# A ring of eight weight slots in place of six for the experts of a two-block model, with the item loop written out for four placements

## The reference, cut to what matters

```
logits = h @ router_w + router_b               # 256 tokens, 32 experts
top_val, top_idx = top_k(logits, 4)            # 4 experts a token
gate = softmax(top_val)
for each expert e, for its tokens x:
    gu  = x @ w_gu[e] + b_gu[e]                # 1024 -> 2048
    g, up = split(gu); g = min(g, 7); up = clip(up, -7, 7)
    act = (up + 1) * (g * sigmoid(1.702 * g))
    y[token] += gate * (act @ w_down[e] + b_down[e])   # 1024 -> 1024
h = h + g2 * rmsnorm(y, ffn_post_g)
```

## Time and profile before

| | us |
|---|---|
| median of 3 runs (lowest, highest) | 1937.54 (1937.01, 1938.84) |
| the profiled execution's own time | 1938.65 |
| its span | 1936.9 |
| TensorE busy | 1864.7 |
| VectorE busy | 768.5 |
| ScalarE busy | 231.1 |
| GpSimd busy | 207.3 |
| data moved by the DMA queues | 558.10 MB, mean 288 GB/s |

### The profile page before, as it was taken

One profiled execution on the slowest core, in us unless ns is written; L12 is line 12 of the kernel. 1 busy time (PEld: TensorE's weight loads), 2 busy tenths in 40 slices (PEclk: granted clock), 3 DMA queues, 4 the chain that ended last, 5 costly groups with the idle time before them and its releaser, 6 DMA issues.

```text
span 1936.9 us, 23084 instructions
## 1 busy us (share of the span) xinstructions
PE 1864.7 (96%) x8340; PEld 912.3 (47%) x8340; DVE 768.5 (40%) x1594; ACT 231.1 (12%) x466; POOL 207.3 (11%) x397
## 2 busy tenths in 40 slices
PE   7999999999999999999999999999999999999996
PEld 4466777754667777655433333323323333332332
DVE  3553111145535773395633323323223323332334
ACT  1421000014110000231110000000000000000001
POOL 0200000002006868321000000000000000000000
PEclk9999999999999999999899999999999999999999
DMA  8143343241448865225399999999997499999995
GB/s 310 65 172 117 152 159 147 109 186 65 174 189 323 326 264 199 87 87 228 152 428 428 429 429 428 428 428 429 428 429 292 202 429 429 428 428 428 429 429 236
DMA packets 40910, 558.10 MB, mean 288 GB/s; under 512 B 4534, under 2 KB 5430, under 8 KB 6364
## 3 DMA queue, kind: packets, MB, share of 16 engines
q1 hardware_dynamic: 40380, 556.06, 69.5%
q10 hardware_dynamic: 480, 1.37, 0.2%
HBM read 556.35 MB, written 1.06 MB: 288 GB/s over the span
## 4 chain that ended last, share of the span: by engine, by line
PE 65%; DMA 23%; DVE 9%; issue 2%; ACT 1%; POOL 0%; SPq 0%; ACTq 0%; DVEq 0%; POOLq 0%
DMA ring<-in_exp_w 23%; PE PS L1746 15%; PE PS L2048 15%; PE PS L1474 8%; PE PS L1765 8%; PE PS L2079 6%; PE PS L1651 3%; PE PS L1936 1%; PE PS L2034 1%; PE PS L2056 1%; DVE ring L1151 1%; DVE tT L1389 1%; DVE tT L1392 1%; DVE tb L1393 1%; DVE tb L1390 1%
## 5 line engine op out<-in xcount | busy, mean ns | idle before, releaser
L2048 PE MATMUL PS<-ring,tb 128*64 128x512 f32 x2176 | 481.5, 595 | 22.7 <-POOLq L2188 20.2
L2048 PEld LDWEIGHTS PS<-ring,tb 128*64 128x64 f32 x2176 | 150.5, 137 | 349.5 <-issue 295.8
L1746 PE MATMUL PS<-hT,ring 128*128 128x256 f32 x1376 | 300.6, 379 | 0.0
L1746 PEld LDWEIGHTS PS<-hT,ring 128*128 128x128 f32 x1376 | 261.1, 190 | 43.0 <-issue 8.6
L2079 PE MATMUL PS<-ring,tb 128*64 128x512 f32 x1088 | 241.0, 595 | 3.7
L1474 PE MATMUL PS<-ring,hT 128*128 128x512 f32 (+2 forms) x448 | 187.6, 561 | 3.4 <-ACT hT L420 3.3
L1389 DVE TENSOR_SCALAR tT<-PS 128x512 f32<-128x512 f32 x34 | 23.5, 692 | 397.5 <-PE PS L2056 397.5
L1765 PE MATMUL PS<-ring,tT 128*128 128x512 f32 x352 | 154.7, 593 | 0.0
L2079 PEld LDWEIGHTS PS<-ring,tb 128*64 128x64 f32 x1088 | 77.7, 137 | 145.1 <-issue 143.9
L1078 DVE TENSOR_TENSOR tT<-PS,tT 128x512 f32<-128x512 f32 x22 | 15.2, 692 | 270.3 <-PE PS L1746 270.3
L1474 PEld LDWEIGHTS PS<-ring,hT 128*128 128x128 f32 x448 | 81.7, 192 | 72.2 <-issue 60.0
(11 more groups left out here) (449 smaller groups left out, 1584.5 us busy)
## 6 DMA issues: line engine op xcount, KB each, us to landing
ring<-in_exp_w SPq DMA_DIRECT2D x192, 2048.0 KB, 21.2
ring<-in_w_gate_up SPq DMA_DIRECT2D x22, 2048.0 KB, 8.5
ring<-in_ada_w SPq DMA_DIRECT2D x12, 2048.0 KB, 9.3
ring<-in_w_in_part SPq DMA_DIRECT2D x10, 2048.0 KB, 10.1
ring<-in_w_down SPq DMA_DIRECT2D x10, 2048.0 KB, 7.3
ring<-in_w_out SPq DMA_DIRECT2D x6, 2048.0 KB, 8.6
ring<-in_w_in SPq DMA_DIRECT2D x4, 2048.0 KB, 8.1
ring<-in_w_in_part SPq DMA_DIRECT2D x2, 1608.0 KB, 11.8
```

What stands on the lines that cost most here:

```text
L1746: ins = pe.matmul(PS[:, 4 + 2 * (i % 2) + part, 256 * f:256 * f + 256], wt[:, k, 256 * part + 128 * f:256 * part + 128 * f + 128], hT[:, k ...
L2048: ins = pe.matmul(PS[64 * h:64 * h + 64, b, :], xg[:, o:o + 64], ring[:, s, w:w + 512], start=k == 0, stop=False, skip_group_check=True)
```

## The change

1. `ring`, `xn` and `proj` become one tensor `mega`, one behind the other, under their old names. The first 32768 columns are eight places of 4096: six are the ring, the seventh covers `xn` and the first 2048 columns of `proj`, the eighth the next 4096 columns of `proj`. The regions inside `proj` change their order: `post`, then `g_row`, then `p2`.
2. Load s of expert e goes to place (6e + s) mod 8. The pattern repeats after four experts. The load before it in that place is slot (s + 4) mod 6 of expert e - 1, or of e - 2 for s = 0 and 1, and SP waits for that one to be freed. SP also waits until the previous load counted on the same semaphore has landed. SP's loop over the experts is written out.
3. Expert 1's load 0 is issued once the S5 gate's products are through and expert 0's load 0 has landed; its load 1 after the bias product L2023, the item counts, and a copy by POOL of the second half of `g_row` to a free part of the constants (`g_ffn`), from where the final norm now reads it.
4. TensorE's loop becomes an outer loop of eight trips over four copies of the item's code, one for each expert mod 4; each copy is an inner loop from the item count of the expert before to that of the expert, and both are read from the table with `value_load`.
5. Other users of the memory move: the squares' scratch output goes to `junk` in the constants and later to `tb`, the gathered rows `xr` to `par`, the comparison for the items' experts is made in two halves in `tmp`, the total is read from `item_i[95]`, and `item_i[63]` becomes 0. The `idle_products` read another part of the constants.

```
+        mega = sb("mega", [P, 4096 * RING + TT * D + TT * IN_W])
+        ring = mega[:, 0:4096 * RING].rearrange("p (s n) -> p s n", s=RING)
...
+        def slot_of(r, s):
+            at = 4096 * ((6 * r + s) % SLOTS)
+            return mega[:, at:at + 4096]
...
-            expert(0, 0)
+            for s in FIRST_ORDER:
+                sp.wait_ge(freed[s], USES_BEFORE[s] + 1)
+                sp.dma_start(slot_of(0, s), a["exp_w"][0, s]).then_inc(landed[s], 16)
+            sp.wait_ge(g.pe2, PE2["gl_p"] + 1)
+            sp.wait_ge(landed[0], 16 * LOADS_BEFORE[0] + 16)
+            sp.dma_start(slot_of(1, 0), a["exp_w"][1, 0]).then_inc(landed[0], 16)
+            sp.wait_ge(g.pe2, PE2["m_bd"] + 1)
+            sp.wait_ge(g.u_pa, 7)
             sp.wait_ge(g.dve2, DVE2["m_cnt"] + 1)
-            with sp.Fori(1, N_EXPERTS) as e:
-                expert(e, sp.value_load(item_i[0:1, bass.ds(e + ENDS_AT - 1, 1)], min_val=1, max_val=MAX_ITEMS))
+            sp.wait_ge(landed[1], 16 * LOADS_BEFORE[1] + 16)
+            sp.dma_start(slot_of(1, 1), a["exp_w"][1, 1]).then_inc(landed[1], 16)
...
+            for e in range(1, N_EXPERTS):
+                before, done = done, items_until(e - 1)
+                for s in range(2 if e == 1 else 0, RING):
+                    last = (s + 4) % RING
+                    sp.wait_ge(freed[last], (before if s < 2 else done) + (USES_BEFORE[last] + 1))
+                    sp.wait_ge(landed[s], 16 * (e + LOADS_BEFORE[s]))
+                    sp.dma_start(slot_of(e % SLOT_TURNS, s), a["exp_w"][e, s]).then_inc(landed[s], 16)
...
-            with pe.Fori(0, items) as n:
+            def item(n, r):
...
+            def items_until(e):
+                return pe.value_load(item_i[0:1, bass.ds(e + ENDS_AT, 1)], min_val=0, max_val=MAX_ITEMS)
+            with pe.Fori(0, N_EXPERTS // SLOT_TURNS) as m:
+                for r in range(SLOT_TURNS):
+                    with pe.Fori(items_until(SLOT_TURNS * m + (r - 1)), items_until(SLOT_TURNS * m + r)) as n:
+                        item(n, r)
...
+            pool.wait_ge(g.dve2, DVE2["s5_d"] + 1)
+            link.to(pool.tensor_copy(g_ffn, g_row[:, 1024:2048]), g.u_pa, 7)
```

More of the change, by code:

```diff
@@ L153 @@
 FIRST_ORDER = (3, 2, 4, 5, 0, 1)
+SLOTS, SLOT_TURNS = 8, 4
 def last_plan():
@@ L273, in program @@
         pf = proj[:, :, :].rearrange("p t c -> p (t c)")
-        p2 = pf[:, 0:Q_N]
-        g_row = pf[:, Q_N:Q_N + 2048]
-        post = pf[:, Q_N + 2048:Q_N + 4096]
+        post = pf[:, 0:2048]
+        g_row = pf[:, 2048:4096]
+        p2 = pf[:, 4096:4096 + Q_N]
+        g_ffn = K[:, K_DEC:K_DEC + 1024]
+        junk = K[:, K_DEC + 1024:K_DEC + 1536]
         ssm = tbf[:, 0:2048].rearrange("p (i n) -> p i n", i=4)
@@ L385, in _ @@
                     sp.dma_start(bias_in.rearrange("p (h t) -> p h t", h=NH), rows).then_inc(g.s_b2, 16)
[L387 to L391, removed]
-            expert(0, 0)
-            sp.wait_ge(g.dve2, DVE2["m_cnt"] + 1)
-            with sp.Fori(1, N_EXPERTS) as e:
-                expert(e, sp.value_load(item_i[0:1, bass.ds(e + ENDS_AT - 1, 1)], min_val=1, max_val=MAX_ITEMS))
+            for s in FIRST_ORDER:
[6 more added lines that the diff above has]
+            sp.wait_ge(g.u_pa, 7)
+            sp.wait_ge(g.dve2, DVE2["m_cnt"] + 1)
+            sp.wait_ge(landed[1], 16 * LOADS_BEFORE[1] + 16)
+            sp.dma_start(slot_of(1, 1), a["exp_w"][1, 1]).then_inc(landed[1], 16)
+            def items_until(e):
+                return sp.value_load(item_i[0:1, ENDS_AT + e:ENDS_AT + e + 1], min_val=1, max_val=MAX_ITEMS)
+            done = None
+            for e in range(1, N_EXPERTS):
[5 more added lines that the diff above has]
+                    sp.dma_start(slot_of(e % SLOT_TURNS, s), a["exp_w"][e, s]).then_inc(landed[s], 16)
             for t in range(TT):
@@ L651, in mixed_squares @@
                 s = st[:, 246 + 2 * t + nh:247 + 2 * t + nh]
-                link.to(nc.scalar.activation(xn[:, t, 512 * nh:512 * nh + 512], PS[:, 2 + 2 * t + nh, :], ACT.Square, accum_out=s),
+                link.to(nc.scalar.activation(junk, PS[:, 2 + 2 * t + nh, :], ACT.Square, accum_out=s),
                         g.act2, ACT2[f"w_s1_{t}"] + nh + 1)
@@ L658, in residual_squares @@
                     s = st[:, 250 + 2 * t + nh:251 + 2 * t + nh]
-                    link.to(nc.scalar.activation(xn[:, t, 512 * nh:512 * nh + 512], x[:, t, 512 * nh:512 * nh + 512], ACT.Square, accum_out=s),
+                    link.to(nc.scalar.activation(junk, x[:, t, 512 * nh:512 * nh + 512], ACT.Square, accum_out=s),
                             g.act2, ACT2[f"w_s2_{t}"] + nh + 1)
@@ L686, in _ @@
             act.wait_ge(g.dve2, DVE2["m_cnt"] + 1)
-            items = act.value_load(item_i[0:1, 63:64], min_val=N_EXPERTS, max_val=MAX_ITEMS)
+            items = act.value_load(item_i[0:1, ENDS_AT + 31:ENDS_AT + 32], min_val=N_EXPERTS, max_val=MAX_ITEMS)
             with act.Fori(0, items) as n:
@@ L701, in _ @@
                 act.wait_ge(g.m_f, t + 1)
-                nc.scalar.activation(xn[:, t, :], oacc[:, t, :], ACT.Square, accum_out=st[:, 230 + t:231 + t]).then_inc(g.m_fs, 1)
+                nc.scalar.activation(tbf[:, 1024 * t:1024 * t + 1024], oacc[:, t, :], ACT.Square, accum_out=st[:, 230 + t:231 + t]).then_inc(g.m_fs, 1)
         @block.vector
@@ L1355, in _ @@
             modulated(link, 1)
[L1357 to L1360, removed]
+            half = MAX_ITEMS // 2
+            below = tmp[:, 512:512 + 32 * half].rearrange("p (j e) -> p j e", j=half)
+            for j in (0, half):
+                link(v.tensor_tensor(below, tmp[:, 32:64].unsqueeze(1).broadcast_to([P, half, 32]),
+                                     K[:, K_IOTA + j:K_IOTA + j + half].unsqueeze(2).broadcast_to([P, half, 32]), ALU.is_le))
+                link(v.tensor_reduce(owner[:, j:j + half], below, AX_X, ALU.add))
             link(v.tensor_scalar(owner, owner, float(N_EXPERTS - 1), None, ALU.min))
@@ L1363, in _ @@
             link.to(v.tensor_copy(item_i[:, MAX_ITEMS:MAX_ITEMS + 1], owner[:, MAX_ITEMS - 1:MAX_ITEMS]), g.dve2, DVE2["m_tab"] + 1)
-            items = v.value_load(item_i[0:1, 63:64], min_val=N_EXPERTS, max_val=MAX_ITEMS)
+            items = v.value_load(item_i[0:1, ENDS_AT + 31:ENDS_AT + 32], min_val=N_EXPERTS, max_val=MAX_ITEMS)
             expert_row(ch, 0, 1)
@@ L1409, in _ @@
                 v.wait_ge(g.m_f, t + 1)
[L1410 removed]
+            v.wait_ge(g.u_pa, 7)
+            link(v.tensor_tensor(tmp[:, 0:1024], oacc[:, 0, :], g_ffn, ALU.mult))
             v.wait_ge(g.m_fs, 2)
@@ L1813, in idle_products @@
                 for _ in range(n):
-                    pe.matmul(PS[:, bank, :], ident, K[:, K_FLIP:K_FLIP + 512], start=True, stop=True)
+                    pe.matmul(PS[:, bank, :], ident, K[:, K_ONE:K_ONE + 512], start=True, stop=True)
             pe.wait_ge(g.act2, ACT2["n_xa"] + 1)
@@ L2027, in _ @@
             pe.wait_ge(g.dve2, DVE2["m_cnt"] + 1)
-            items = pe.value_load(item_i[0:1, 63:64], min_val=N_EXPERTS, max_val=MAX_ITEMS)
+            items = pe.value_load(item_i[0:1, ENDS_AT + 31:ENDS_AT + 32], min_val=N_EXPERTS, max_val=MAX_ITEMS)
             def scatter_half(t, value):
@@ L2047, in _ @@
                                 w = 2048 * kk + 1024 * b + 512 * h
-                                ins = pe.matmul(PS[64 * h:64 * h + 64, b, :], xg[:, o:o + 64], ring[:, s, w:w + 512],
+                                ins = pe.matmul(PS[64 * h:64 * h + 64, b, :], xg[:, o:o + 64], slot_of(r, s)[:, w:w + 512],
                                                 start=k == 0, stop=False, skip_group_check=True)
@@ L2079, in _ @@
                         ins = pe.matmul(PS[64 * h:64 * h + 64, 2, :], aT[:, P * (c % 4) + 64 * (c // 4):P * (c % 4) + 64 * (c // 4) + 64],
-                                        ring[:, s, o:o + 512], start=c == 0, stop=c == KC - 1, skip_group_check=True)
+                                        slot_of(r, s)[:, o:o + 512], start=c == 0, stop=c == KC - 1, skip_group_check=True)
                     if c == 3:
@@ L2182, in _ @@
             pool.wait_ge(g.dve2, DVE2["m_tab"] + 1)
-            items = pool.value_load(item_i[0:1, 63:64], min_val=N_EXPERTS, max_val=MAX_ITEMS)
+            items = pool.value_load(item_i[0:1, ENDS_AT + 31:ENDS_AT + 32], min_val=N_EXPERTS, max_val=MAX_ITEMS)
             with pool.Fori(1, items) as n:
```

12 lines of the change are left out of this document (6 added, 6 removed).

## The result

The changed kernel takes 1919.51 us (median of 4 runs, 1918.97 to 1922.74) against 1937.49 (a fourth run joined the three above): ratio 0.9909, 95% interval 0.9897 to 0.9921. The forecast was 1920, with a range of 1915 to 1934. Its profiled execution took 1919.41 us with a span of 1917.4, 19.2 and 19.5 under those of before.

A forecast was written before the change was run, and what follows sets the result against it. Expert loop bound by a race of TensorE and DMA weight loads. Profiled execution 1938.65 - 18 (less lateness) + 0.3 (loop exits) = 1920.9; median 1919.8, called 1920; range 1915 to 1934.

The forecast's parts named there:

- Two candidates, a race in two stretches: Expert loop: DMA needs 29.37 us an expert, TensorE 27.55 an item; 29.0 us lateness, 18.8 before item 19, 10.2 after.
- first stretch: Expert loop up to item 18: loads start earlier, the stream is 9.0 us sooner, lateness falls from 18.8 to 9.8 us.
- second stretch: Expert loop after the long DMA idle window: two more loads in memory give 9.8 us lead against 10.2 lost; 0.4 left.
- The entry: TensorE's start of the expert loop: two more reads and loop set-up delay item 0's products by 2.0 us, to 957.5.
- Reads and branches hidden: Each expert's end: 2.1 us more sequencer work hides under its 4.05 us lead, leaving 1.9; cost nothing.
- Instruction fetch: TensorE's loop of four copies stays resident, cost nothing; otherwise 0 to 5.8 us at each of seven outer back edges.
- the break-even of 0.87 us an expert: Each expert's end: unhidden register work above 0.87 us an expert would make the change a slowdown; chance 0.07.
- the limit of TensorE's pace: Expert loop: with TensorE setting the pace throughout, the last product ends at 1893.2 plus all costs inside the loop.
- the rival filed as a faster 1929: TensorE's outer back edges fetch instructions: at 2.5 us an edge, 9.0 us later than forecast, 1929; chance 0.19.
- rival C: Loop entry: the clock falls while TensorE idles 2.6 us, item 0 loses about 5 us, total 1924; chance 0.06.
- The sum: Whole expert loop: lateness 9.8 + 0.4 = 10.2 in place of 29.0, -18.8 us; taken as -18.
- the schedule's 17.6: Expert loop carried item by item with the same constants: gives -17.6 us, reproducing the present end 0.9 us short.

The follow-up runs named there:

- six_places: The changed kernel with six places again and none of expert 1's loads issued before item 0 frees a slot: 1941.24 us, ratio 1.0015 to the kernel before.
- pair_late: The changed kernel with expert 1's loads 0 and 1 issued only when item 0 has freed slot 0, with load 2: 1931.7 us, ratio 0.9964.
- short_fifth: The changed kernel with slot 5's load of experts 1 to 31 cut to 128 of 4096 columns, no candidate: 1910.23 us, ratio 0.9856.
- after_again: The changed kernel run once more, unaltered, for a second profile and time: 1919.75 us, ratio 0.9906.
- reads_3: The changed kernel with three more unused item-table reads by TensorE's sequencer ahead of each expert's inner loop: 1925.06 us, ratio 0.9933.
- reads_moved: The changed kernel with TensorE's read of the item total moved after the loop and each inner loop's start taken from a register: 1921.23 us, ratio 0.9916.
- reads_5: The changed kernel with five more unused item-table reads by TensorE's sequencer ahead of each expert's inner loop: 1939.25 us, ratio 1.0002.
- eight_copies: The changed kernel with the item's code written out eight times in place of four, some 2300 instructions: 1930.0 us, ratio 0.9962.
- halves: The changed kernel with each load from expert 1 on split into two of 2048 columns, freed and awaited by halves: 1930.95 us, ratio 0.9963.
- by_partitions: The changed kernel with each load from expert 1 on split into two transfers of 64 partitions, rows whole: 2794.07 us, ratio 1.4433.

## Why the prediction was right

*Two candidates, a race in two stretches.* The mechanism is right: six places, the late pair and the short loads show both parts, and that what is left is the loads' pace. The sizes have to be compared with care. The forecast counts both from the old start of the loop: 9.0 us sooner at item 19, 18.8 at item 33. Measured are 10.5 (1517.25 to 1506.72) and 19.4 (1913.09 to 1893.66). The 10.2 us of lateness above are counted from this kernel's own start, so that they equal the forecast's 10.2 is a coincidence; counted from the old start they would be 9.6. Since 2.0 us of the gain lie ahead of the loop, the change itself brought 8.5 us in the first stretch (9.0 forecast) and 8.9 in the second (9.8 forecast).

The first stretch: item 0 started at 954.8 in place of the forecast's 957.5, 2.0 us of that ahead of the loop, so load 2 was issued at 958.5 and not at 961.3. But it took 8.3 us to land where the forecast took 7.7, and from item 0's start to the landing of load 5 it was 27.3 us, not 26.2.

The second stretch: the stream of loads loses time that the forecast does not have. In the stream of loads after the long idle stretch one load lands 5.6 us after its forerunner and not 4.9; it is load 0 of expert 30, here with the load ahead of it (issue at 1805.4 and at 1813.4, then the time to landing), and the queue that fetches instructions for the engines other than TensorE, in 1838 to 1839:

```profile
L417 SPq DMA_DIRECT2D mega<-in_exp_w x1: 327/327/327, 1805.4 to 1805.4; - x1
DMA to landing us min/median/max: 29.3/29.3/29.3
...
L417 SPq DMA_DIRECT2D mega<-in_exp_w x1: 328/328/328, 1813.4 to 1813.4; - x1
DMA to landing us min/median/max: 26.9/26.9/26.9
```
```profile
q14 instruction: 1, 0.01, 2.0%
```

A second, smaller step (5.2 us, expert 24's load 1, which lands at 1668.4) has such a block beside it too, in 1666 to 1668.5. Together they are 1.0 us. The larger step stands at the same load in the profiles of after_again, pair_late, reads_3 and reads_moved, and at the next load in that of six_places; the kernel before, whose loop on SyncE is not written out, fetches no such block after 966 and has no such step after the stream starts again. That fetches for SyncE's written-out loop delay the loads fits all of this, but no run tests it.

*The entry.* The term was mis-sized: item 0 starts 1.36 us later by it, not 2.0. I took 0.9 us for each further read where it is at most 0.77, and no cover, though in the kernel before TensorE ended its idle time at the entry by waiting for DVE. It has no place of its own in the sum; it acts through item 0's start, on which the issue of load 2 hangs.

*Reads and branches hidden.* Right, and shown with its limit: 2.7 us left after both reads (1.9 forecast), three more hidden, five not. The time of the five reads is that of the kernel before within 0.1%, but that is not the break-even of 0.87 us an expert that was forecast: only 0.6 us an expert come to light, and the rest is the longer entry (5.17 us idle) with its fall of the clock.

*Instruction fetch.* Right in what happens here, wrong in the price of the rival. I gave an outer edge 0 to 5.8 us and took 2.5; the edges of eight copies cost 5 to 7 each with the clock. By the limit of TensorE's pace seven of those are 35 to 49 us, and the products would have ended at 1893.2 + 35 = 1928 at the earliest, 26 us behind the forecast's 1902: the rival filed as a faster 1929 was, by this estimate, a slowdown to 1946 or more. My forecast had its sign safe only as long as the four copies stay resident.
On the rule of the Trainium skill, "Runtime: NRT & Kernel Launch", Instruction fetch mechanics: the trace agrees with the room for 2048 instructions (four copies, by my count some 1200 instructions, are not fetched again; eight, some 2300, are), and disagrees with a window of two pages for TensorE: the four copies are some five blocks, and their back edge takes 216 ns.

*The clock at the entry* (rival C, 0.06). It did not fall in either profile of the changed kernel, but it did in that of short_fifth, with the same 1.9 us of idle time, and in those of reads_3 and reads_5, with 3.9 and 5.2 us. Its price of 4 us was too high (1.7 us in short_fifth, 2.5 in reads_3). Other profiles with the changed kernel's entry (six_places, pair_late, eight_copies) show no fall, so 0.06 was small but not refuted.

*The sum.* 1920.9 us were forecast for the profiled execution, 1919.4 measured. Of the 19.2 us of gain, 2.0 lie ahead of the loop and were luck; the change's own part is some 17.4, where the sum had 18 - 0.3 = 17.7. This close agreement is partly luck too: the two stretches added up to 18.8, which is 1.4 too much, and what made it good was the choice of a round 18 between that and the schedule's 17.6.

## What to carry to other kernels

Where transfers and TensorE are within a few per cent of each other, read the loss as lateness against the faster pace, split at the places where the queue runs empty: an earlier start pays in the first stretch, more places in the next, and they add (9.9 + 8.9 us here). Count lateness from one and the same start when two kernels are compared. A sequencer's register work is free up to the lead that it has over its array, which the timeline shows as the distance from a loop's first register instruction to its first product. Before code is written out, count its instructions: here a loop that fitted cost its sequencer 0.2 us an edge, hidden, and one that didn't cost TensorE 5 to 7.

## What the runs showed of the hardware

- A back edge whose target is no longer resident held TensorE's sequencer 5.9 to 6.6 us with a busy DMA (eight_copies); resident it is 0.2 (the changed kernel).
- Reads of SBUF by TensorE's sequencer run beside queued products, 304 ns each in a loop, 484 to 494 for the first one of an execution.
- Loads in halves, with rows of 8 KB in place of 16 KB and twice the transfers, go with 422 in place of 428 GB/s at full DMA engines (halves); transfers into 64 partitions in place of 128 move 215 (by_partitions).
- The clock's fall at a given idle stretch differs between executions: 10.2 us of half clock from 937.8 in the profile of before, 6.8 us from 936.4 in the one of after, both beginning inside the same gap of 3.20 us.
